# The low halves of the third slot's weight pieces on GpSimd, in an RWKV-7 inference step

## The reference

```
k = xk @ w_k ; v = xv @ w_v
decay = exp(-exp(-softplus(-(w0 + tanh(xw @ w1) @ w2)) - 0.5))
a = sigmoid(a0 + (xa @ a1) @ a2)
kk = k * k_k, normalised per head of 64 ; k = k * (1 + (a - 1) * k_a)
per token: Sa = S . a_t ; S = S * w_t + Sa b_t + v_t k_t ; y = S . r_t      (32 heads, 64 x 64 state each)
out = (groupnorm(y) + bonus) * g @ w_o
```

## Time and profile before

| | us |
|---|---|
| median of 3 runs | 2713.64 (2710.94 to 2715.29) |
| the profiled execution | 2709.54 |
| its span, first to last instruction | 2708.0 |
| PE busy | 2584.9 (95%) |
| DVE busy | 1583.1 (58%) |
| ACT busy | 1127.6 (42%) |
| POOL busy | 142.2 (5%) |

### The profile page before, as it was taken

The page is one execution under the profiler, slowest core; times in us unless marked ns, Lnnn a source line. Parts: engine busy times, 40 slices in busy tenths (PEclk is TensorE's granted clock), DMA queues, the critical chain, the costliest instruction groups (busy, mean ns, idle before and its releaser), DMA issues.

```text
span 2708.0 us, 56286 instructions
## 1 busy us (share of the span) xinstructions
PE 2584.9 (95%) x23289; PEld 2475.8 (91%) x23289; DVE 1583.1 (58%) x2411; ACT 1127.6 (42%) x1580; POOL 142.2 (5%) x211
## 2 busy tenths in 40 slices
PE   7979999999999899999999999969999999999997
PEld 6977878888788799999999999958999999999997
DVE  6877878888856644444444444586444444444446
ACT  4564555555433533333333333445333333333334
POOL 1000111111101100000000000100000000000000
PEclk9999999999999999999999999979999999999999
DMA  7532323222335666556665556624565566565563
GB/s 227 155 84 69 83 83 82 75 79 81 97 99 165 166 168 168 160 144 167 185 169 166 161 144 167 180 73 116 163 170 160 145 166 186 165 170 161 144 166 94
DMA packets 707051, 379.30 MB, mean 140 GB/s; under 512 B 16023, under 2 KB 699191, under 8 KB 706711
## 3 DMA queue, kind: packets, MB, share of 16 engines
q1 hardware_dynamic: 701040, 363.42, 48.0%
q0 software_dynamic: 5792, 13.34, 1.9%
q10 hardware_dynamic: 70, 0.39, 0.1%
HBM read 367.28 MB, written 10.62 MB: 140 GB/s over the span
## 4 chain that ended last, share of the span: by engine, by line
PE 80%; DVE 13%; ACT 4%; issue 2%; DMA 0%; DVEq 0%; SPq 0%; ACTq 0%; POOL 0%
PE PS L708 24%; PE PS L709 24%; PE PS L710 24%; PE PS L855 2%; DVE WL L1647 2%; ACT WH L1225 1%; DVE PL L1749 1%; DVE TM L1791 1%; DVE TM L1655 1%; DVE ML L1662 1%; PE PS L887 1%; ACT PH L1318 1%; DVE XL L1887 1%; PE PS L725 1%; PE PS L929 0%
## 5 line engine op out<-in xcount | busy, mean ns | idle before, releaser
L1647 DVE TENSOR_TENSOR WL<-RAW,WH 128x2048 fp32r<-128x2048 f32 (+1 forms) x325 | 658.6, 2027 | 764.4 <-ACT WH L1225 764.4
L708 PE MATMUL PS<-MH,WH 128*128 128x288 f32 (+1 forms) x3152 | 933.3, 296 | 25.0 <-DVE ML L2046 11.8
L709 PE MATMUL PS<-ML,WH 128*128 128x288 f32 (+1 forms) x3152 | 934.7, 297 | 0.0
L710 PE MATMUL PS<-MH,WL 128*128 128x288 f32 (+1 forms) x3152 | 933.7, 296 | 0.0
L1225 ACT ACTIVATE WH<-RAW 128x2048 fp32r<-128x2048 f32 (+1 forms) x325 | 553.3, 1702 | 822.8 <-PE PS L710 808.4
L708 PEld LDWEIGHTS PS<-MH,WH 128*128 128x128 f32 (+1 forms) x3152 | 596.3, 189 | 31.1 <-issue 20.1
L709 PEld LDWEIGHTS PS<-ML,WH 128*128 128x128 f32 (+1 forms) x3152 | 596.6, 189 | 0.2
L710 PEld LDWEIGHTS PS<-MH,WL 128*128 128x128 f32 (+1 forms) x3152 | 595.9, 189 | 0.0
L709 PE MATMUL PS<-HL,WH 128*128 128x288 f32 x1408 | 415.3, 295 | 0.0
L710 PE MATMUL PS<-HH,WL 128*128 128x288 f32 x1408 | 415.0, 295 | 0.0
L708 PE MATMUL PS<-HH,WH 128*128 128x288 f32 x1408 | 413.4, 294 | 0.0
(11 more groups left out here) (304 smaller groups left out, 2718.7 us busy)
## 6 DMA issues: line engine op xcount, KB each, us to landing
RAW<-in_ffn_w_in SPq DMA_DIRECT2D x176, 1024.0 KB, 5.7
RAW<-in_ffn_w_down SPq DMA_DIRECT2D x128, 704.0 KB, 4.8
RAW<-in_rw_wr SPq DMA_DIRECT2D x16, 1024.0 KB, 6.1
PR<-in_rw_wk SPq DMA_DIRECT2D x64, 256.0 KB, 3.1
PR<-in_rw_wv SPq DMA_DIRECT2D x64, 256.0 KB, 3.1
PR<-in_rw_wo SPq DMA_DIRECT2D x64, 256.0 KB, 3.3
S0N<-in_state_wkv POOLq DMA_DIRECT2D x64, 64.0 KB, 2.4
out<-SOS POOLq DMA_DIRECT2D x64, 64.0 KB, 2.7
```

The lines of the kernel that those rows point to most:

```text
L708: pe.matmul(out, wh, xh, start=first, stop=False)
L709: pe.matmul(out, wh, xl, start=False, stop=False)
L710: return pe.matmul(out, wl, xh, start=False, stop=last)
L1647: dve.tensor_tensor(WL[0:rows, j % 2, 0:n], RAW[0:rows, j, 0:n], WH[0:rows, j % 2, 0:n].bitcast(F32), ALU.subtract).then_inc(lo_ready, 1)
```

## The change

The low halves of slot 2 (pieces 2, 5 and 8 of each p) are made by GpSimd instead of VectorE. They have a semaphore of their own, pc_lo_pool; pc_lo keeps the other six of each p. GpSimd's loop is written out turn by turn, p = 0 to 15: before the SOS stores of turn p comes the low half of piece 2 of p+2, after them that of piece 5, after the state loads that of piece 8. The wait for the SOP store moves into the next turn. Where VectorE begins its unit steps, it waits for all of GpSimd's low halves and adds their number to pc_lo, so that the counts of the units stay as they were.

```diff
+        def lo_by(p, j):
+            return (pc_lo_pool, p * 3 + j // 3) if j % 3 == 2 else (pc_lo, p * 6 + 2 * (j // 3) + j % 3)
+        def lo_kept(e):
+            return (pc_lo_pool, 3 * KC + 1) if e == 2 else (pc_lo, 6 * KC + 1 + e)
...
 @@ SyncE, fetch(p)
-                    sp.wait_ge(pc_lo, p * PIECES + (j + 1))
+                    signal, q = lo_by(p, j)
+                    sp.wait_ge(signal, q + 1)
 @@ SyncE, the units' fetches
-                sp.wait_ge(pc_used if 3 <= e < SLOTS else pc_lo, free_after(e))
+                if e < 3:
+                    sp.wait_ge(*lo_kept(e))
+                else:
+                    sp.wait_ge(pc_used if e < SLOTS else pc_lo, free_after(e))
...
 @@ GpSimd
+            def piece_lo(p, j):
+                if p < KC:
+                    pool.wait_ge(pc_hi, p * PIECES + (j + 1))
+                    pool.tensor_tensor(PL[2][:, :], PR[2][:, :], PH[2][:, :].bitcast(F32), ALU.subtract)\
+                        .then_inc(pc_lo_pool, 1)
...
             pool.wait_ge(slab_used, 2 + SLAB["ffn0"])
             states(pairs[0], 0)
+            piece_lo(0, 2)
+            piece_lo(0, 5)
             pool.wait_ge(xkept, 16)
             pool.wait_ge(mixlo_ready, MIXED)
             states(pairs[1], 0)
-            with pool.Fori(0, KC // 2 - 1) as i:
-                for z in pairs:
-                    results(z, i, True)
-            for z in pairs:
-                results(z, KC // 2 - 1, False)
+            piece_lo(0, 8)
+            for j in (2, 5, 8):
+                piece_lo(1, j)
+            for p in range(KC):
+                z, i = pairs[p % 2], p // 2
+                piece_lo(p + 2, 2)
+                if p:
+                    prompt_stored(pairs[(p - 1) % 2], (p - 1) // 2)
+                sample_states(z, i)
+                piece_lo(p + 2, 5)
+                pool.wait_ge(z.stored, 80 * i + 64)
+                if i + 1 < KC // 2:
+                    states(z, i + 1)
+                piece_lo(p + 2, 8)
+                prompt_state(z, i)
+            prompt_stored(pairs[1], KC // 2 - 1)
 @@ TensorE, arrived(j)
-                        pe.wait_ge(pc_lo, p * PIECES + (j + 4))
+                        signal, q = lo_by(p, j)
+                        pe.wait_ge(signal, q + (2 if j % 3 == 2 else 3))
 @@ VectorE, piece_lo
                 slot = j % 3
+                if slot == 2:
+                    return
 @@ VectorE, units
+                dve.wait_ge(pc_lo_pool, 3 * KC + 1)
+                dve.sem_inc(pc_lo, 3 * KC + 1)
                 unit_lo(2)
```

More of the change, by code:

```diff
@@ L324, in build @@
         pc_lo = sem("pc_lo")
+        pc_lo_pool = sem("pc_lo_pool")
         pc_used = sem("pc_used")
@@ L601, in _ @@
             pool.sem_inc(hl_ready, 2)
-            pool.sem_inc(pc_lo, 3)
+            pool.sem_inc(pc_lo, 2)
+            pool.sem_inc(pc_lo_pool, 1)
             pool.sem_inc(pc_used, 3)
@@ L629, in states, with sample_states @@
                                        src.rearrange("v b h k -> v b (h k)")).then_inc(z.s0in, 16)
[L631 to L634, removed]
+            def piece_lo(p, j):
[3 more added lines that the diff above has]
+                        .then_inc(pc_lo_pool, 1)
+            def sample_states(z, i):
+                pool.wait_ge(z.act.sem, z.act.value("sos", i))
                 for b2 in range(2):
@@ L640, in results, with prompt_state, prompt_stored @@
                                        z.SOS[b2 * HN:(b2 + 1) * HN, :, h * HN:(h + 1) * HN]).then_inc(z.stored, 16)
[L641 to L646, removed]
+            def prompt_state(z, i):
+                pool.wait_ge(z.act.sem, z.act.value("sop", i))
                 pool.dma_start(wkv_p[0, 0][bass.ds(4 * i + 2 * z.b, 2), :, :].rearrange("h v k -> (h v) k"), z.SOP[:, :])\
                     .then_inc(z.stored, 16)
+            def prompt_stored(z, i):
                 pool.wait_ge(z.stored, 80 * i + 80)
```

## The result

The changed kernel takes 2755.81 us (median of 4 runs, 2753.25 to 2761.03) against 2714.3 us (4 runs of the kernel before beside it): 1.0158 times as long, 95% interval 1.014 to 1.0175. The forecast was 2761 us. The profiled execution of the changed kernel is the longest of its runs, 2761.03 us with a span of 2759.2 us, 51.2 us more than the span before.

What follows compares the result with a forecast made beforehand. The RWKV stage was taken as TensorE-bound (463.1 of 480 us busy). 14 x (0.56 + 2.71) = 45.8, + 1 = 47 us more, 2761 us on the median of 2713.64; range 2738 to 2796.

Steps and rivals of the forecast that it cites:

- Piece 5: Its low half queues behind four SOS stores on GpSimd; TensorE stands 2.71 us longer in each of 14 turns.
- the stores: Within piece 5's wait: GpSimd issues four SOS stores before the low half, 2.50 us.
- the piece: Within piece 5's wait: one 128x512 low half on GpSimd, 1.3 us alone.
- the first issue: Within piece 5's wait: from SOS's end to GpSimd's first store issue, 0.6 us.
- the contention term: GpSimd's low half takes 0.4 us more beside a VectorE instruction with two SBUF inputs; counted on pieces 2 and 5.
- handing on: Allowance for passing GpSimd's finished low half on, 0.05 us, an estimate.
- Piece 2: GpSimd needs 1.82 us after the high half where 1.26 are available; TensorE is late by 0.56 us a turn.
- The prediction's other-side rival: TensorE loses nothing, VectorE's relief shrinks the waits for XL and TT (6.9 + 2.0 us): 2705 us; chance 0.04.
- The clock: Rival: each turn's TensorE pause also halves the granted clock, 1.5 us in all 14 turns, 21 us, 2782; chance 0.2.
- The start: Pieces of p = 0 and 1 have no SOS before them and the stage isn't yet TensorE-bound: 0.
- The hand-over: TensorE's first unit after the last piece waits for a count from VectorE's first unit step: 1 us, bounds 0 and 1.5.
- Hidden parts: Piece 8's later fetch, landing and low half, and the state loads, cost TensorE nothing.

Runs made afterwards that it cites:

- The pair of runs with piece 5 alone: The changed kernel with only piece 5's low half on GpSimd, ahead of the SOS stores (2707.07 us) or behind them (2743.44 us).
- extra subtractions: The kernel before, GpSimd's program written out, plus 42 128x512 GpSimd subtractions nobody waits for; VectorE still makes all low halves: 2739.13 us, 1.0106.
- piece 8 alone: The changed kernel with only piece 8's low half on GpSimd, behind the next state loads; VectorE makes pieces 2 and 5: 2721.25 us, 1.0033.
- piece 5 alone ahead of the stores: The changed kernel with only piece 5's low half on GpSimd, ahead of the SOS stores; VectorE makes pieces 2 and 8: 2707.07 us, 0.9981.

## Why the prediction was right

**Piece 5 (2.71 us forecast).** Right in place and mechanism, 2.10 us in size (4.24 - 2.14). Its terms: the stores 2.50, measured 2.51; the piece 1.3, measured 1.28; the first issue 0.6, measured 0.30; the contention term 0.4, measured 0 on GpSimd; handing on 0.05, measured 0.14. The first-issue lag had been read at p = 14, where the loop has ended but the wait still goes through a register (`to_reg`), as it does in the loop. In the written-out program it is 0.29 us in the same turn. That SOS moves with TensorE, so that every turn pays again, held in all 14. The pair of runs with piece 5 alone shows this term by itself, with its clock: 35.6 us, where the whole change costs 41.5.

**Piece 2 (0.56 us forecast).** TensorE starts 1.40 us after the high half in place of 1.26: 0.14 us. The error is again the 0.4 of contention. It pointed the wrong way: I had read the 1.19 and 1.86 us sums of the earlier trace rows as GpSimd held by VectorE. That reading was right for them (the low half at 882.30 starts 0.16 us before the sum), but here GpSimd starts first and VectorE is held, on the low half of piece 3 (0.68 to 1.35 us).

**Contention.** No term of the sum had a VectorE instruction grow. In the changed kernel this is mostly covered, because TensorE waits for piece 5 while R<-R,TM is held. Where the cover is gone it costs 27 us (extra subtractions) or 10 us (piece 8 alone, in its place). The prediction's other-side rival, VectorE's relief at 2705 us, leaves this out. With piece 5 alone ahead of the stores, where its condition holds, the time is 2707 us, but of the two waits only TT's went; XL's stayed at 0.49 us a turn.

**The clock.** The rival said 1.5 us in all 14 turns. The profiled execution shows 1.45 us (39.12 - 37.67) behind 7 of 14 pauses, the last of them behind the last piece 5. So forecast and rival share the result. For the 14 turns: 14 x (37.67 - 35.53) = 30.0, + 6 x 1.45 = 8.7 of clock, + 1.3 for one turn with a late store issue, + 1.2 for the first of them, which is 3.4 us longer than before = 41.2, against 41.1 measured. The forecast's 45.8 came near by luck: terms that were too large (0.3 of first issue, 0.4 of contention twice, some 15 us in 14 turns) stood for 11 us of clock, late store and first turn that it had not counted. On the medians the change costs 41.5 us, where the forecast had 47. The other three executions of the changed kernel are 4.8 to 7.8 us shorter than the profiled one, at a mean clock that is 0.002 to 0.004 higher; how many stretches at 0.50 they have is not on record. With a pause of 0.95 us (one of 2.26 makes the mean 1.07) the clock fell behind none of the pauses at piece 5. The one stretch, at 333.31, follows waits of 0.49 and 0.89 us for XL and U.

**The start (0 forecast).** 4.6 us. The step that failed is "the stage isn't yet TensorE-bound there: 0": there TensorE waits for what VectorE makes, the mixes and BK, and VectorE is held. The pause of TensorE is 1.32 us at 175.27 where it was 0.40, and TensorE's wait for BK, 4.17 us before, is 5.5 us. Not all of the 4.6 is this. TensorE is 0.8 us late at 168.92 already, before GpSimd's first low half, and from BK's wait to piece 5 of p = 1 it loses 1.4 us, in a stretch at 0.50 that lasts 6.8 us from 202.62 where before it lasted 3.4 from 200.52. Two executions whose programs are the same up to there (piece 5 alone, ahead and behind) differ by 1.1 us at this point.

**The hand-over (1 forecast).** 0.72 us of waiting for L2014. Each run that removed it changed something else too, so its price alone was not measured.

**Hidden parts.** Piece 8's landing is now what its high half waits for (3.38 us at 565.68 in the turn above), and behind it ScalarE still waits 1.17 us for TensorE before the root: hidden, as said. VectorE "33 us less busy" is wrong; it is 8 us busier. The turn of 38.5 to 39 us is right as a mean only, 38.59.

## What to carry to other kernels

Moving an instruction to an idle engine moves it into that engine's queue: what stands ahead of it, and what that waits for, is its real start time. Here the order of two calls decided between 1.2% slower and 0.2% faster. Then look at what the other engine runs while it is there: a GpSimd subtraction of 1.28 us cost a short VectorE instruction of the critical chain up to 2 us, and it may not show until a longer wait that covers it is gone.

## What the runs showed of the hardware

- GpSimd's 128x512 subtraction takes 1.28 us and a 128x512 copy 0.63 us where VectorE does not hold it. Beside the subtraction some VectorE instructions are held to its end: R<-R,TM (two SBUF inputs) from 0.46 to 2.01 us, SPD (a tensor_scalar from SBUF, 128x64) from 0.21 to 2.07. What one loses is the time to GpSimd's end, whatever its own length. Instructions with an input from PSUM are not stretched (XL takes 0.42 us beside the subtraction and 0.41 elsewhere), nor is the reciprocal, with one SBUF input (1.95 us at most, beside it and elsewhere).
- VectorE's instruction loses even when it starts first, if GpSimd comes straight from its own DMA issues: R<-R,TM starts 0.36 to 0.49 us before the subtraction in the changed kernel and beside the extra subtractions, SPD up to 0.85 us before, each while GpSimd still issues DMAs with the subtraction next in its queue. SPD then ends 0.06 us after GpSimd's end. The Trainium skill, "SBUF — State Buffer", section "Who interferes with whom", states that VectorE with two SBUF inputs or in a two-port mode shares a port pair with GpSimd, and that whoever issues first has it for the whole instruction. That one is fully blocked agrees with the 2.07 us. The order of starts in the trace does not agree in these cases (a start in the trace need not be the moment of issue), and the measurement decides.
- Where GpSimd comes from a wait on a semaphore and VectorE starts first, if only by 0.12 us, VectorE wins, and here the order of starts does agree. The 1.19 us sum of the earlier trace rows is such a case. In the run with extra subtractions both engines wait for the same high half, and GpSimd's takes 1.73 us in place of 1.28, then VectorE's second of two is held (2.41 us for both, 1.29 in the earlier trace rows):

```profile
574.95 1.73 POOL L639 TENSOR_TENSOR DUM<-CW 128x512 f32<-128x512 f32 x1 [7.14 <-ACT PH L1335]
```
```profile
574.83 2.41 DVE L1766 TENSOR_TENSOR PL<-PR,PH 128x512 fp32r<-128x512 f32 x2 [0.83 <-ACT PH L1335]
```

- DMA issues alone do not do this. In the kernel before, where GpSimd has only these in the turns, SPD's mean is 234 ns (the longest 0.40 us) and that of R<-R,TM 458:

```profile
L1928 DVE TENSOR_SCALAR SPD<-ST,PC 128x64 f32<-128x64 f32 x48 | 11.2, 234 | 0.1
L1780 DVE TENSOR_TENSOR R<-R,TM 128x288 f32<-128x288 f32 x16 | 7.3, 458 | 0.5
```

- One and the same 2.2 us pause was followed by the clock at 0.50 in half the turns and by 1.00 in the others of one execution. What tells them apart was not tried.
- In the kernel before, where the wait for SOS goes through a register, the first store is issued 0.76 to 0.95 us after SOS's end within the loop and 0.56 to 0.60 us after it where the loop has ended. In the written-out program it is 0.29 us in nearly every turn.
